# A low-rank gate unit with the high and low words of its 16 columns side by side, and two products in place of three

## The reference

```python
h = rms_norm(x, p['norm1_g'])
proj = h @ p['w_in']
gq, gk, gv, gr, ga, rq, rk, rv, rg, xq, gates = jnp.split(proj, split_at, axis=-1)   # ga has 16 columns
log_a = jax.nn.log_sigmoid((ga @ p['gla_a_up'] + p['gla_a_b']).astype(jnp.float32)) / GLA_TAU
```

## Time and profile before

| | |
|---|---|
| median of three runs | 1187.25 us |
| profiled execution, its time | 1188.98 us |
| profiled execution, its span | 1187.2 us |
| TensorE busy | 1147.5 us, 97% |
| ScalarE, GpSimd, VectorE busy | 578.8, 761.7, 534.1 us |
| mean granted TensorE clock | 0.993 of full |

### The profile page before, as it was taken

How to read it: one execution, slowest core, us unless ns; L and a number is a source line. 1 busy time by engine, 2 the same in 40 slices (tenths; PEclk the granted TensorE clock), 3 DMA queues, 4 the chain that set the end, 5 groups by cost and what they waited for, 6 DMA issues and landing times.

```text
span 1187.2 us, 24480 instructions
## 1 busy us (share of the span) xinstructions
PE 1147.5 (97%) x8652; PEld 1102.4 (93%) x8652; DVE 534.1 (45%) x1064; ACT 578.8 (49%) x1028; POOL 761.7 (64%) x592
## 2 busy tenths in 40 slices
PE   5999999999999999999999999999999999999995
PEld 4897899999999999999989878999999999999995
DVE  5346233243866551255152642324267665315523
ACT  6464354455347663344455634455444566434431
POOL 3664556666776777777676545566577677777772
PEclk9999999999999999999999999999999999999997
DMA  7754545444554445455566455544454454454551
GB/s 277 250 190 162 178 145 173 153 144 154 169 143 145 153 145 156 144 153 154 149 209 210 169 187 182 163 152 151 121 165 144 142 146 154 143 154 148 147 161 45
DMA packets 53211, 190.79 MB, mean 161 GB/s; under 512 B 6032, under 2 KB 7312, under 8 KB 52880
## 3 DMA queue, kind: packets, MB, share of 16 engines
q1 hardware_dynamic: 43632, 159.15, 43.8%
q10 hardware_dynamic: 9504, 30.56, 7.0%
HBM read 181.15 MB, written 8.53 MB: 160 GB/s over the span
## 4 chain that ended last, share of the span: by engine, by line
PE 90%; DVE 5%; DMA 2%; issue 1%; ACT 1%; POOL 1%; SPq 0%; DVEq 0%; ACTq 0%; POOLq 0%
PE bank L1048 46%; PE bank L1079 30%; PE bank L1090 7%; DMA raw<-w 2%; PE bank L1295 1%; DVE arena L683 1%; DVE arena L773 1%; PE bank L1286 1%; PE bank L1173 1%; PE bank L1162 1%; PE bank L1191 1%; PE bank L1305 1%; PE bank L1275 1%; POOL wlo L252 1%; DVE arena L810 1%
## 5 line engine op out<-in xcount | busy, mean ns | idle before, releaser
L252 POOL TENSOR_TENSOR wlo<-raw,whi 128x512 fp32r<-128x512 f32 x588 | 761.5, 1316 | 406.0 <-PE bank L1079 191.9
L287 ACT ACTIVATE whi<-raw 128x1024 fp32r<-128x1024 f32 x294 | 311.0, 1058 | 295.1 <-PE bank L1048 165.3
L1079 PE MATMUL bank<-oh,whi 128*128 128x320 f32 x848 | 267.4, 315 | 3.5 <-DVE arena L942 2.1
L1079 PE MATMUL bank<-oh,wlo 128*128 128x320 f32 x848 | 262.0, 309 | 0.0
L1079 PE MATMUL bank<-ol,whi 128*128 128x320 f32 x848 | 262.0, 309 | 0.0
L1048 PE MATMUL bank<-hh,whi 128*128 128x320 f32 x832 | 257.6, 310 | 0.0
L1048 PE MATMUL bank<-hl,whi 128*128 128x320 f32 x832 | 257.1, 309 | 0.0
L1048 PE MATMUL bank<-hh,wlo 128*128 128x320 f32 x832 | 257.1, 309 | 0.0
L1079 PEld LDWEIGHTS bank<-oh,whi 128*128 128x128 f32 x848 | 159.2, 188 | 11.9 <-issue 5.4
L1079 PEld LDWEIGHTS bank<-ol,whi 128*128 128x128 f32 x848 | 159.3, 188 | 0.3
L1079 PEld LDWEIGHTS bank<-oh,wlo 128*128 128x128 f32 x848 | 159.2, 188 | 0.0
(11 more groups left out here) (186 smaller groups left out, 1335.5 us busy)
## 6 DMA issues: line engine op xcount, KB each, us to landing
raw<-w SPq DMA_DIRECT2D x296, 512.0 KB, 3.6
arena<-cache_k ACTq DMA_DIRECT2D x16, 512.0 KB, 6.1
arena<-cache_v ACTq DMA_DIRECT2D x16, 512.0 KB, 5.3
arena<-st_in ACTq DMA_DIRECT2D x8, 512.0 KB, 5.5
sst_out<-arena ACTq DMA_DIRECT2D x8, 512.0 KB, 4.2
con<-consts SPq DMA_DIRECT2D x1, 1284.0 KB, 13.5
x<-x_in SPq DMA_DIRECT2D x2, 640.0 KB, 10.5
arena<-mem_in SPq DMA_DIRECT2D x2, 512.0 KB, 6.4
```

Of the source, the lines that this page charges most:

```text
L252: i = pool.tensor_tensor(out=wlo[:, s % 2, h], in0=raw[:, s, h], in1=whi[:, s, h].bitcast(f32), op=ALU.subtract)
L287: nc.scalar.activation(whi[:, s, :], raw[:, s, :], ACT.Copy).then_inc(hi_ready, 1)
L1079: r = MM(o, a, b[:, k, 0:n], start=k == 0 and i == 0, stop=k == KT_ - 1 and i == 2, skip_group_check=True)
```

## The change

Unit 9's weights now stand twice in the padded tile, in columns 0 to 15 and again in columns 16 to 31. After GpSimd has made the low words, ScalarE copies the low words of columns 16 to 31 (8 pieces of 16, one for each 128 rows of the weight) over the high words in `whi`. The stationary tile then holds high words in 16 columns and low words in the next 16, so that one product with `oh` and one with `ol` give all the terms, in separate rows of the result. The rows of `gla_a_up` are doubled in `par` too, so that L1140 adds both halves up. TensorE waits for a new counter, `ga_ready`, before the first product of unit 9. The term low weight by low activation, which was left out before, is now in the sum.

```diff
+        ga_ready = sem("low_rank_words_together")
...
                 if not lv:
                     normed_hi(5, 6, 7)
                     act.wait_ge(rmt_ready, 1)
+                act.wait_ge(lo_ready, lv * UNITS + U_GA + 1)
+                words = [w_.rearrange("p (k c) -> p k c", c=P)[:, :, LOWRANK:2 * LOWRANK] for w_ in (whi[:, U_GA % 4, :], wlo[:, U_GA % 2, :])]
+                nc.scalar.activation(words[0], words[1].bitcast(f32), ACT.Copy).then_inc(ga_ready, 1)
                 done(U_MV + 3)
                 hi(U_MV + 7)
...
                 for i in range(4):
                     vunit(U_MV + i, i, hh, hl, (0, P), B)
-                unit(U_GA, oh, ol, T, (hl_ready, lv * 16))
+                wait_bank(U_GA)
+                ready(U_GA)
+                pe.wait_ge(ga_ready, lv + 1)
+                for k in range(KT_):
+                    pe.wait_ge(hl_ready, lv * 16 + k + 1)
+                    for j, y in enumerate((oh, ol)):
+                        r = MM(A[U_GA % 2][:, 0:T], whi[:, U_GA % 4, k * P:(k + 1) * P], y[:, k, :], start=k == 0 and j == 0,
+                               stop=k == KT_ - 1 and j == 1, skip_group_check=True)
+                r.then_inc(unit_done, 1)
...
-    par[0:LOWRANK, C_AU:C_AU + 256] = a["gla_a_up"][i]
+    par[:, C_AU:C_AU + 256] = np.pad(np.tile(a["gla_a_up"][i], (2, 1)), ((0, P - 2 * LOWRANK), (0, 0)))
...
-    ga[:, :LOWRANK] = col["ga"]
+    ga[:, :2 * LOWRANK] = np.tile(col["ga"], (1, 2))
```

## The result

The changed kernel takes 1195.82 us (median of four runs, 1193.97 to 1197.37) against 1187.24: a ratio of 1.0063, 95% interval 1.0051 to 1.0076. It is slower by 8.6 us; forecast was 1193.6, between 1190.0 and 1196.3.

The account below looks back on a forecast made before the run. TensorE, busy 97% of the span, was taken as the bound. Late starts of 1.72 and 1.48 us plus 3.1 us of half clock gave +6.3 us on 1187.25, stated as 1193.6, range 1190.0 to 1196.3.

Parts of the forecast that it names:

- Where the copy stands: ScalarE's queue: copy behind the last normed tile in layer 0, 0.96 us behind the start of unit 11's conversion in layer 1.
- That the removal gains nothing where it stands: Unit 9: sixteen products, at most 2.35 us, almost worthless in layer 0 where tiles pace; L1140 waits for L381 in layer 1.
- rival C: Both layers, loads early: the sixteen products count in full, TensorE 2.35 us sooner, 1184.9 us; chance 4%.
- The late start: Unit 9's first product at 50.34 in layer 0 and 627.13 in layer 1, costing 1.48 and 1.72 us.
- The clock: TensorE after the idle stretches of 5.3 and 3.65 us: half clock costs 1.55 us in each layer, 3.1 in all.
- the whole unit: Upper bound of the half-clock cost: all 16 products of unit 9 at half clock in both layers, 3.8 us.
- rival A: Unit 9 in both layers: same delays but clock stays at 1.00, +3.2 us, 1190.4 us; chance 13%.
- The sum: Whole kernel: 1.72 for layer 1, 1.48 for layer 0 and 3.1 for the clock, +6.3 us.
- the forecast's own bounds: Total time of the changed kernel under the main forecast, 1192 to 1195 us; that forecast's chance 66%.
- rival D: Behind unit 9: later waits grow longer or half clock lasts twice as long, 3.1 us more, 1196.7 us; chance 9%.
- B: Units 10 and 11: loads land early enough that the copy isn't late, about 1187.1 us, no change; chance 8%.

Follow-up runs that it names:

- two products alone: Changed kernel without the copy and TensorE's wait for it, weights' low words left out and high words counted twice: 1188.59 us, ratio 0.9999.
- the wait alone: Kernel before with all 24 products, plus the copy into a buffer that nothing reads and TensorE's wait for it: 1195.56 us, ratio 1.0059.
- the last run above: Kernel before with three products and a wait for a copy nobody reads, its result spread over 8 pieces 288 bytes apart: 1197.05 us.

## Why the prediction was right, point by point

**Where the copy stands.** Right in both layers; moving it took all of the loss away (1.0004), and taking the late loads away took it too (0.9977).

**That the removal gains nothing where it stands.** Right: 0.9999 for two products alone. In the profile of that run 1.3 us of half clock in layer 0 work against the products, so a gain below about 1 us is not ruled out; rival C's 2.35 is.

**The late start.** The first product was expected at 50.34 and came at 51.09. Two small terms were missed: unit 10's load landed 0.45 us later (its conversion is at 44.97 for 44.52 before), and the release was taken as 0.05 us, from L1140 behind L381, where 0.35 and 0.30 were measured. Layer 1's pause was 4.03 for 3.65: the release took 0.25 us more than assumed, and unit 11's conversion stood 0.14 us later behind unit 8's end.

**The clock.** "I take 1.55 for each layer, 3.1 us in all" is the mis-sized term: 2.43 and 1.60, so 4.0. In layer 0 half clock covered all of unit 9 and three products of unit 10 (51.09 to 56.3), beyond the bound of "the whole unit". Layer 1's estimate was right. But one size for each pause there is not: taken in the same way, against 5.87 us (7.04 for twice 24 products, 2 x 3.52), such pauses cost 1.60 us in layer 1 with the copy early in layer 0, 1.90 and 1.62 with the wait alone, and 2.61 and 2.51 in the last run above. Both idle stretches were followed by half clock, and rival A's 1190.4 is out. The rule of the Trainium skill that was weighed there ("TensorE: Matmul & The Clock Gate", section "What's actually happening": the throttled clock is the default and activity releases it) agrees with that. A restart at half clock in both layers is not what the rows show: layer 1's unit 9 ran its first six products at full pace.

**The sum.** In the profiles layer 0 is 4.66 us late (L1152 at 59.39 for 54.73) in place of 1.48 + 1.55, and layer 1 adds 3.7 (unit 8 ends 4.76 late, at 628.24, and L1152 is 8.45 late) in place of 1.72 + 1.55. 1.48 + 0.45 + 0.30 + 2.43 = 4.66. And 1.72 + 0.4 for the longer pause + 1.60 = 3.7. Nothing of it was made up or added later: 8.45 at L1152 of layer 1, 8.3 at the end. The median, 1195.82, lies inside the stated range but above the forecast's own bounds of 1192 to 1195, on the side of rival D, whose half clock of double length was nearly true in layer 0 (2.43 us for 1.55). That the range held owes something to its having been drawn up towards D.

**Rivals.** B and C had their condition tried, the loads early. With the loads behind the store of the memory values, the kernel with the change and the one without end level, as B had it (1185.63 and 1186.1), and for B's reason: TensorE waits for L381's counterpart in layer 1 in both (0.48 and 0.83 us). With the loads' issuing moved behind that copy too, the change gained 1.4 us in the profiles. C's 2.35 were not reached: the unit's later start took 0.44 and 0.34 us, and a wait of 0.15 us ahead of unit 10 in layer 1 the rest. (B's 0.7 us for unit 10's earlier start in layer 1 is 0.9 by its own rows, 627.11 - 626.18; nothing hangs on it.)

## What to carry to other kernels

A small operation put into an engine's queue takes the place's lateness with it: look not at its 0.3 us but at what stands ahead of it there in the profile, and at whether the waiting engine waits for that today. A transfer's delay that costs nothing (ScalarE's 4 to 6 us of idleness here) becomes the path's as soon as something urgent stands behind it; moving the transfer or the operation are both cures, and the first may be worth more than the change. Savings on the bounding engine count only where nothing else ends at the same time; here they were worth nothing that could be measured in one arrangement and about 1.5 us in another.

## What was not expected of the hardware

The half clock between the layers is in three of the thirteen profiles (the kernel before, the changed one, and the changed one with the cache loads behind the store) and absent in ten, though the pauses ahead of it are the same in all (0.81 to 0.83 and 1.35 or 1.36 us). One row, of the kernel with the early copy:

```profile
600.00:606.00 6.00, 4.90 (x38) 4.77 (x39) 1.54 (x4) 2.15 (x3) 5.17 (x5) 1.00 0.72 210
```

Its clock stays at 1.00, where it is 0.50 from 601.1 to 604.2 in the earlier trace rows. From L1140 in layer 0 to the end of unit 8 in layer 1 the three with half clock take 568.8 to 568.9 us, the others 567.3 to 567.7: about 1.5 us a time. Such pauses that sometimes bring the clock down and sometimes not may be a good part of why runs of one kernel differ by 2 to 3 us. The 61 runs of the kernel before beside the experiments agree with that: the 21 whose mean granted clock was 0.996 have a median of 1187.7 us, the 18 at 0.993 or 0.994 one of 1189.2. It was not tested by itself. Issuing four cache loads kept ScalarE for 3.58 us in one place (from 48.77 with the loads moved behind the store), where it took 2.01 in another (before, from 614.41).
